# A fused decoder layer: a third projection unit in the opening, two reordered lists, one earlier subtraction

## The reference, cut to what matters

```python
mod = silu(c) @ w_ada + b_ada
shift1, scale1, gate1, shift2, scale2, gate2 = split(mod, 6)
h = rms_norm(x) * (1 + scale1) + shift1
gq, gk, gv, g_lr, g_gate, hq, hf, hi, h_gate = split(h @ w_in)
log_a = log_sigmoid(g_lr @ gate_w2 + gate_b2) / 16
o_gla  = chunk_gla(gq / 8, gk, gv, log_a, 64)
o_hgrn = chunk_gla(silu(hq), 1 - forget(hf), hi, log(forget(hf)), 64)
y = concat(rms_norm(o_gla) * silu(g_gate), rms_norm(o_hgrn) * silu(h_gate)) @ w_out
x = x + gate1 * y
h = rms_norm(x) * (1 + scale2) + shift2
x = x + gate2 * (square(relu(h @ w_mlp1)) @ w_mlp2)
return rms_norm(x) * final_norm_g
```

## Time and profile before

| | us |
|---|---|
| median of 3 runs | 1164.33 (1163.85 to 1164.86) |
| the profiled execution | 1163.81, span 1162.1 |
| PE busy | 1135.4 (98%) |
| DVE busy | 865.3 (74%) |
| ACT busy | 612.4 (53%) |
| POOL busy | 494.9 (43%) |
| DMA | 186.73 MB, 161 GB/s on the mean |
| mean granted PE clock | 0.995 of full |

### The profile page before, as it was taken

How to read it: one execution, slowest core, us unless ns; L and a number is a source line. 1 busy time by engine, 2 the same in 40 slices (tenths; PEclk the granted TensorE clock), 3 DMA queues, 4 the chain that set the end, 5 groups by cost and what they waited for, 6 DMA issues and landing times.

```text
span 1162.1 us, 15677 instructions
## 1 busy us (share of the span) xinstructions
PE 1135.4 (98%) x5555; PEld 939.4 (81%) x5555; DVE 865.3 (74%) x1044; ACT 612.4 (53%) x933; POOL 494.9 (43%) x320
## 2 busy tenths in 40 slices
PE   7999999989999999999999999999999999999996
PEld 7788788777878788888888888888888888788886
DVE  6898887587778677377976775677795884966876
ACT  7763555756566566255654555455664433524424
POOL 1021122134243345336534343344566675665751
PEclk9999999999999999999999999999999999999999
DMA  9777387344353546722445344544624637447203
GB/s 356 263 234 272 129 202 209 79 127 134 92 173 100 155 122 213 241 77 82 143 156 184 142 156 125 182 145 159 195 64 161 220 92 264 150 133 278 71 1 145
DMA packets 162949, 186.73 MB, mean 161 GB/s; under 512 B 7604, under 2 KB 119352, under 8 KB 159928
## 3 DMA queue, kind: packets, MB, share of 16 engines
q1 hardware_dynamic: 160472, 179.44, 46.7%
q0 software_dynamic: 2400, 6.29, 2.8%
HBM read 138.51 MB, written 40.89 MB: 154 GB/s over the span
## 4 chain that ended last, share of the span: by engine, by line
PE 92%; DVE 2%; DMA 2%; ACT 2%; SPq 1%; issue 1%; DVEq 0%; ACTq 0%
PE unit_bank L1764 19%; PE unit_bank L2178 9%; PE unit_bank L2180 9%; PE unit_bank L2179 9%; PE small_bank L2178 9%; PE small_bank L2180 9%; PE small_bank L2179 9%; PE small_bank L1764 4%; PE unit_bank L2025 3%; PE unit_bank L2027 3%; PE unit_bank L2026 3%; PE small_bank L1901 2%; DMA ada_slot<-in_w_ada_dram 2%; PE small_bank L1803 1%; PE small_bank L1893 1%
## 5 line engine op out<-in xcount | busy, mean ns | idle before, releaser
L1016 POOL TENSOR_TENSOR wr_lo<-quarter,wr_hi 128x512 fp32r<-128x512 f32 x122 | 197.2, 1628 | 174.6 <-ACT wr_hi L1552 174.4
L2178 PE MATMUL unit_bank<-op_hi,wr_hi 128*128 128x512 f32 x452 | 176.8, 391 | 0.9 <-issue 0.9
L2180 PE MATMUL unit_bank<-op_hi,wr_lo 128*128 128x512 f32 x452 | 176.0, 389 | 0.0
L2179 PE MATMUL unit_bank<-op_lo,wr_hi 128*128 128x512 f32 x452 | 176.0, 389 | 0.0
L2178 PE MATMUL small_bank<-op_hi,wr_hi 128*128 128x512 f32 x448 | 174.6, 390 | 0.0
L2179 PE MATMUL small_bank<-op_lo,wr_hi 128*128 128x512 f32 x448 | 174.4, 389 | 0.0
L2180 PE MATMUL small_bank<-op_hi,wr_lo 128*128 128x512 f32 x448 | 174.4, 389 | 0.0
L1552 ACT ACTIVATE wr_hi<-wr_full 128x512 fp32r<-128x512 f32 x90 | 56.8, 631 | 174.8 <-DVE wr_full L2921 174.8
L2921 DVE TENSOR_TENSOR wr_full<-quarter,quarter 128x512 f32<-128x512 f32 x90 | 89.1, 991 | 56.8 <-PE small_bank L2180 22.9
L1552 ACT ACTIVATE wr_hi<-quarter 128x512 fp32r<-128x512 f32 x136 | 82.9, 626 | 89.3 <-PE unit_bank L2180 49.1
L1764 PE MATMUL unit_bank<-a_hi,w_hi 128*128 128x512 f32 x304 | 121.1, 398 | 0.0
(11 more groups left out here) (370 smaller groups left out, 2382.5 us busy)
## 6 DMA issues: line engine op xcount, KB each, us to landing
quarter<-in_w_mlp_dram SPq DMA_DIRECT2D x128, 256.0 KB, 4.1
hidden_scratch<-hid SPq DMA_DIRECT2D x98, 256.0 KB, 2.3
ada_slot<-in_w_ada_dram SPq DMA_DIRECT2D x48, 512.0 KB, 6.6
op_full<-hidden_scratch SPq DMA_DIRECT2D x21, 1024.0 KB, 4.8
pair_quarter<-in_w_in_dram SPq DMA_DIRECT2D x32, 256.0 KB, 3.6
piece_x<-t_scratch SPq DMA_DIRECT2D x16, 512.0 KB, 4.1
piece_y<-t_scratch SPq DMA_DIRECT2D x32, 256.0 KB, 3.4
raw<-in_w_out_dram SPq DMA_DIRECT2D x16, 512.0 KB, 3.9
```

The costliest lines, as they stand in the source:

```text
L1016: pool.tensor_tensor(wr_lo[slot][:, :, :], split_source(n), wr_hi[slot][:, :, :].bitcast(F32), ALU.subtract).then_inc(wr_lo_pool, 1)
L2178: pe.matmul(dst, wh, ah, start=opens, stop=False, skip_group_check=True)
L2179: pe.matmul(dst, wh, al, start=False, stop=False, skip_group_check=True)
L2180: mm = pe.matmul(dst, wl, ah, start=False, stop=k == KH - 1, skip_group_check=True)
```

## The change

Unit 2's weight is loaded early, behind the ninth piece of `w_ada`, into `w_full` (the place of `w_lo[0]`, which nothing has used by then). POOL copies it into `w_hi[0]`, which rounds it, in the place of ACT's rounding; POOL's low part reads `w_full` and waits until DVE has made the low parts of all 16 input tiles. On PE the opening adds for the tiles 0 to 3 two products for unit 2 (high x high and high x low), in `SB[2]` and `SB[3]`; the rest of the unit (its tiles 4 to 7, and low x high of 0 to 3, `third_unit_end`) is made in P0. The "z" products move to the banks 0 and 1. On DVE `pack_gate` and `low_weights_first(1)` stand behind add 8 in place of add 9. On ACT the two copies of unit 2's banks stand ahead of the gate's exponential: one more than before is in front of it (`read_out(0)` was there already, the copy `copy_out(t1, 0)` comes from behind the logarithm).

In the first pair `keys(0)` stands ahead of `pair_high(early, P6)`, and the rounding `t4_hi` (`high_fourth`) moves from the end of H0 to behind `copy_part(early, 0)`. In all three pairs `low_squares(1)` stands ahead of `q_rel` and `weight_sum_of(late, "S4")`. The counts of some semaphores follow.

```diff
     if own == "P":
-        s[0] += [("z", 0, 0, 2), ("z", 0, 1, 3)]
+        s[0] += [("z", 0, 0, 2), ("z", 0, 1, 3)] if prev else [("z", 0, 0, 0), ("z", 0, 1, 1)]
...
+        w_full = at("w_full", 176, [P, KT, P])
...
+        def third_bank(half):
+            return SB[2 + half][:, :]
...
             for n in range(8, 20):
                 load_ada(n)
+                if n == 8:
+                    sp.dma_start(w_full[:, :, :], w_in[0, :, GQ:GQ + P].rearrange("(k p) m -> p k m", p=P)).then_inc(gain_loaded, 16)
...
             for j, q in enumerate(pair_cols + head_cols):
-                load_unit(2 + j, j % 2, w_in, 0, q)
+                if j:
+                    load_unit(2 + j, j % 2, w_in, 0, q)
...
+            pool.wait_ge(whi_ready, 2)
+            pool.wait_ge(gain_loaded, 16)
+            pool.tensor_copy(w_hi[0][:, :, :], w_full[:, :, :]).then_inc(whi_ready, 1)
             for u in range(2, U_OUT):
+                if u == 2:
+                    pool.wait_ge(lo_dve, 16)
                 low(u, u % 2)
...
-            high_of(2)
             for half in range(2):
                 act.wait_ge(unit_filled[half], 1)
...
                 read_out(0)
                 if own == "P":
+                    if name == "P0":
+                        copy_out(t1, 0)
                     act.wait_ge(z_abs, 2 * gi + 2)
                     act.activation(t0[:, :], t0[:, :], ACT.Exp, scale=-1.0).then_inc(z_exp, 1)
                     act.wait_ge(z_exp, gi + 1)
                     act.activation(t0[:, :], t0[:, :], ACT.Ln, bias=one).then_inc(z_ln, 1)
                     if gi > 0:
                         act.wait_ge(k_end_ready, gi)
-                    copy_out(t1, 0)
                     if name != "P0":
+                        copy_out(t1, 0)
                         next_high(0)
...
-                    act.wait_ge(t_done, T_DONE_0 + 1)
-                    act.wait_ge(sums_added, 96)
-                    act.activation(t4_hi[:, :, :], xs[3][:, :, :], ACT.Copy).then_inc(t_high, 1)
...
-                pair_high(early, P6)
+                if early:
+                    pair_high(early, P6)
                 wait_join(act, early, 0)
                 keys(0)
+                if not early:
+                    pair_high(early, P6)
                 copy_part(early, 0)
+                if not early:
+                    high_fourth()
...
+            def third_unit(half, tiles):
+                for k in tiles:
+                    wh, wl = w_hi[0][:, k, :], w_lo[0][:, k, :]
+                    ah, al = tok(a_hi[:, k], half), tok(a_lo[:, k], half)
+                    product(third_bank(half), wh, ah, k == 0, False)
+                    product(third_bank(half), wh, al, False, False)
+                    if k >= KH:
+                        pe.wait_ge(wlo_ready, 3)
+                        product(third_bank(half), wl, ah, False, False)
+
+            def third_unit_end(half):
+                pe.wait_ge(wlo_ready, 3)
+                for k in range(KH):
+                    mm = product(third_bank(half), w_lo[0][:, k, :], tok(a_hi[:, k], half), False, k == KH - 1)
+                mm.then_inc(unit_filled[half], 1)
...
                             half_unit(u, u, half, a_hi, a_lo, split_ready(0), (k,))
+                        if k4 == 0:
+                            if k == 0:
+                                pe.wait_ge(whi_ready, 3)
+                                pe.wait_ge(read["ada"], half + 1)
+                            third_unit(half, (k,))
...
-                    if not (name == "P0" and j == 0):
-                        half_unit(u0 + j, 1 + j, half, a_hi, a_lo, tiles=range(KH if name == "P0" and jj == 2 else 0, KT))
+                    if name == "P0" and j == 1:
+                        if half:
+                            third_unit(half, range(KH, KT))
+                        third_unit_end(half)
+                    elif not (name == "P0" and j == 0):
+                        half_unit(u0 + j, 1 + j, half, a_hi, a_lo)
...
                     if name == "P0" and p[0] == "z" and p[2] == 1:
-                        half_unit(u0 + 1, 2, 0, a_hi, a_lo, tiles=range(KH))
+                        third_unit(0, range(KH, KT))
...
                 if n == 8:
                     finish_ada(0, 0, 2)
                     finish_ada(0, 1, 3)
-                if n == 9:
                     pack_gate()
                     low_weights_first(1)
...
+                low_squares(1)
                 dve.wait_ge(e_q, gi + 1)
                 dve.wait_ge(q_cum_ready, gi + 1)
                 dve.scalar_tensor_tensor(q_rel[:, :], q_rel[:, :], 0.5, t0[:, :], ALU.mult, ALU.mult).then_inc(q_rel_ready, 1)
                 weight_sum_of(late, "S4")
-                low_squares(1)
```

More of the change, by code:

```diff
@@ L930, in low @@
                 pool.wait_ge(whi_ready, u + 1)
-                pool.tensor_tensor(w_lo[slot][:, :, :], raw[slot][:, :, :], w_hi[slot][:, :, :].bitcast(F32),
+                pool.tensor_tensor(w_lo[slot][:, :, :], (w_full if u == 2 else raw[slot])[:, :, :], w_hi[slot][:, :, :].bitcast(F32),
                                    ALU.subtract).then_inc(wlo_ready, 1)
@@ L1067, in high @@
             def high(u, slot, loads):
-                act.wait_ge(raw_loaded[slot], 16 * loads)
+                act.wait_ge(raw_loaded[slot], 16 * (loads - (u >= 2 and slot == 0)))
                 if not isinstance(u, int) or u >= 3:
@@ L1080, in high_out @@
                 slot = (U_OUT + v) % 2
-                act.wait_ge(raw_loaded[slot], 16 * ((U_OUT + v) // 2 + 1))
+                act.wait_ge(raw_loaded[slot], 16 * ((U_OUT + v) // 2 + slot))
                 if v == 0:
@@ L1188, in unit @@
                     act.wait_ge(unit_filled[half], u0 + j + 1)
-                    return UB[(2 + 2 * j + half) % 4][:, :]
+                    return third_bank(half) if u0 + j == 2 else UB[(2 + 2 * j + half) % 4][:, :]
                 def next_high(j):
@@ L1337, in pair_high, with high_fourth @@
                 act.activation(pw_hi[place][:, :, :], pair_source(prod), ACT.Copy).then_inc(pair_hi, 1)
+            def high_fourth():
+                act.wait_ge(t_done, T_DONE_0 + 1)
+                act.wait_ge(sums_added, 96)
+                act.activation(t4_hi[:, :, :], xs[3][:, :, :], ACT.Copy).then_inc(t_high, 1)
             def copies(gi):
@@ L1770, in half_unit @@
                 if tiles[0] == 0:
-                    if not isinstance(u, int) or u >= 2:
-                        pe.wait_ge(unit_read[half], u - 1)
+                    if u >= 3:
+                        pe.wait_ge(unit_read[half], 1 if u == 4 else u - 1)
                     pe.wait_ge(wlo_ready, u + 1)
@@ L1980, in stage @@
                     elif name == "P0":
-                        kind, count = (("ada", 3), ("ada", 4), ("ada", 1), ("ada", 2))[b]
-                        pe.wait_ge(read[kind], count)
+                        if b < 2:
+                            pe.wait_ge(read["ada"], 3 + b)
+                        else:
+                            pe.wait_ge(unit_read[b - 2], 3)
                     else:
@@ L3192, in first_columns @@
                 dve.wait_ge(squared, squares_done(t, 0))
-                dve.wait_ge(gain_loaded, 16)
+                dve.wait_ge(gain_loaded, 32)
                 dve.tensor_tensor(out_stage[:, t, 0:HALF], y_bank(t, 0), gain[:, 0:HALF], ALU.mult).then_inc(read["y"], 1)
```

## The result

The changed kernel takes 1169.63 us (median of 6 runs, 1167.47 to 1172.01) beside 1164.85 us of the kernel before on the same chip (6 runs). The ratio is 1.0036, 95% interval [1.0025, 1.0048]: 2.9 to 5.6 us slower. The forecast was 1167.2 us, 2.85 slower: the right side and inside the range of 1161.0 to 1169.8, but beyond the forecast's own 1165.7 to 1168.8; the nearest time on record is the third rival's, 1169.0. The profiled execution took 1168.23 us (span 1166.5), 4.42 more than that of before.

A forecast was written before the change was run, and what follows sets the result against it. TensorE's chain of waits was taken as the bound. Opening 2.5, clock 1.0, keys -1.9 and squares 1.25 sum to +2.85 us, so 1167.2 us as a median; range 1161.0 to 1169.8, the forecast's own 1165.7 to 1168.8.

The forecast's parts named there:

- third rival: Low clock behind the adds and at the keys, a 1.6 us copy; 1169.0 us and somewhat more; chance 0.10.
- Opening, PE's side: Opening, TensorE: eight moved products fill waits at no cost, bringing PE 1.81 us earlier to the end of unit 4.
- Opening, VectorE's side: Opening, VectorE: GpSimd's copy, taken as 1.25 us, holds an add, making every tile 0.58 us later.
- Opening, the gate: Opening's gate: later products and two copies delay log-decay and adds 2.5 us; PE stands 3.7 us.
- first rival: Opening, log-decay to difference: the scan runs beside GpSimd, PE loses only 0.5 us; 1164.2 us; chance 0.22.
- The clock behind the stand: Behind PE's stand for the modulation sums: a half-clock stretch costs 1.0 us, ends 0 and 1.7.
- Keys: Start of the pairs: keys ahead of the rounding let P6 start 1.8 us earlier; taken as -1.9 us.
- Squares: Second half of three heads: squares' waits go, but value transposes come 0.42 us later each; +1.25 us.

The follow-up runs named there:

- E9: The changed kernel with ScalarE's two bank copies put behind the logarithm again; 1165.64 us, ratio 1.0007.
- E6: The changed kernel with GpSimd's subtraction for unit 4 made to wait until VectorE's scan is out; 1168.32 us, ratio 1.0032.
- E1: The changed kernel with the lists of keys and squares as before, so the opening's part of the change alone; 1169.51 us, ratio 1.0041.
- E5: The changed kernel with only half 0 of the third unit's tiles 0 to 3 in the opening, half 1 made in P0; 1165.60 us, ratio 1.0005.
- E8: Changed opening with E4's order and VectorE's reads of the sums ahead of P0's scaled queries, changed keys' list, S4 then squares ahead of scaled queries; 1161.40 us.
- E3: The kernel before with only the squares' subtraction moved earlier, in all three pairs; 1166.42 us, ratio 1.0012.
- E10: As E8, but with only half 0 of the third unit in the opening, and squares and S4 as before; 1161.59 us, ratio 0.9967.
- E4: The changed kernel with VectorE's seven adds ahead of the products for the keys, and TensorE's value transposes ahead of the sums'; 1167.14 us, ratio 1.0022.
- E2: The kernel before with only the first pair's list changed: keys ahead of P6's rounding, the 2048-column rounding behind the copy; 1163.39 us, ratio 0.9988.

## Why the prediction was right, and where it was off

The time came out near the end of the range, 0.17 us below it, and beyond the forecast's own. The low clock came in both places, behind the adds and at the keys, as the third rival has it (1169.0, chance 0.10); the delay by the copy that this rival counts on did not. In each place the mechanism is the forecast's, apart from what follows.

**Opening, PE's side: right.** TensorE is at the sums at 93.84 - 3.71 = 90.13 us (90.65 forecast).

**Opening, VectorE's side: the copy over-priced.** GpSimd's copy took 1.69 us, but began at 31.07, 0.43 behind the start of unit 1's subtraction, and ended 0.9 behind its end. It held the second add by 0.34 us, and the adds afterwards are 0.07 late instead of 0.58.

**Opening, the gate: right in the end, 0.6 smaller, by two paths instead of one.** The absolute value is at 63.88 (64.5), the logarithm ends at 70.38 (71.0), the log-decay starts at 70.42 (71.0). But only the last 0.59 us of it are a wait for the logarithm. VectorE's own list was through with the add ahead of it at 69.83, 1.2 us later than before: it had waited for the first gate product, whose low part it makes at 60.66 instead of 59.56, and the moved products delay that one too. The prediction left VectorE's list where it was and charged the two copies with 1.06; E9 shows 0.7 for them. The scan stood: 4.36 us beside GpSimd's 2.48, and the difference went from 3.23 to 1.22. The block ended 1.95 us late (2.5). The first rival, a scan that runs beside GpSimd, is out by this row and by E6. The stand was 3.71 us (3.7).

**The clock behind the stand: the step that was mis-sized.** The prediction put 1.0 us, with an upper end of 1.7, from a single row of 3.4 us at half clock. It was 6.8 us at 0.50, and TensorE lost 2.2. The end was no bound: it took the length of that one low stretch for the length of any. Nor is 2.2 the price of such a stand: behind stands of 3.70, 3.81 and 1.90 us in E1, E6 and E5 the low stretch was 3.4 us and TensorE lost 1.2 each time, near the forecast. What decides between the two lengths no run here shows.

**Keys: mechanism right, half the gain.** P6 waited 1.35 us for its low part and started when it should (239.31, less the 4.15 of the opening 235.16; 235.2 forecast). Then it ran at the lower clock, which leaves 1.0 of the 1.9 taken; "1.2 us are left" was the prediction's own lower end. Without the low clock it is more: in E8's profile the same place gains 2.4 us.

**Squares: right.** 1.5 us against 1.25, with waits of 1.65 for the values (1.3). E3 shows it alone; there S4 ends 0.40 us later against the operations ahead of it (0.42).

The sum of the terms is then 1.95 + 2.2 - 1.0 + 1.5 = 4.6 instead of 2.85, beside 4.42 between the profiled executions. The timed median of E1 lies 4.8 us over before, its profiled execution only 2.8. Its other runs have a lower mean clock (0.990 to 0.992, the profiled one 0.993), but that explains a part at most: 3.4 us more at 0.50 lower the mean by 0.0015 (3.4 x 0.5 / 1165) and cost up to 1.7 us, and the run with 0.990 is the shortest of the others (1168.52). The rest stays open; no trace shows those runs.

## What to carry to other kernels

Where the critical engine meets another within 0.2 us, work taken off the critical engine's path is worth nothing until the other's list is shortened ahead of that point: look for the meeting point first, and reorder there (E10), then move the work. A wait taken away early can come back as a longer one later, and a stand of TensorE can cost twice, by its length and by the clock behind it; the second part differs from execution to execution, so one trace doesn't price it. A subtraction moved ahead of a transfer's trigger is paid by whoever waits for the landing, even where its own wait was the only one on the list.

## What the runs showed of the hardware

A scan on VectorE stands beside a GpSimd subtraction as a plain two-tile operation does: 4.36 us instead of 2.29. So did a copy of no more than 128x16 in E4: 2.41 us instead of 0.16. The lower clock lasted 6.8 us behind a stand of 3.71 and 3.4 us behind stands of 3.46 (before), 3.70 (E1), 3.81 (E6) and 1.90 (E5), and did not come behind 2.55 in E4 or behind 1.57 and 1.08 in E9. At the keys, with two stands of 1.2 and 1.35 us, it came in the changed kernel, E2 and E10, and not in E8 and E9. The length of the stand alone does not tell. A 256 KB load took 3.8 us instead of 2.9 where a 512 KB one was under way beside it for 3.1 us instead of 1.6; that the one comes from the other is not shown.
